# Two 32-column products in place of one 64-column product in the RWKV inverse of a diffusion trunk step

## The reference

```
sa = s @ kk_t
s  = s * w_t - outer(sa, kk_t * a_t) + outer(v_t, k_t)
y  = s @ r_t
```

## Time and profile before

| | before |
|---|---|
| runs, median (lowest to highest) | 3530.35 us (3522.43 to 3538.04) |
| the profiled execution | 3516.0 us |
| its span | 3514.2 us |
| PE busy, share of the span | 3166.6 us, 90% |
| DVE busy | 1607.5 us, 46% |
| ACT busy | 970.3 us, 28% |
| granted TensorE clock, mean | 0.904 |

### The profile page before, as it was taken

The page is one execution under the profiler, slowest core; times in us unless marked ns, Lnnn a source line. Parts: engine busy times, 40 slices in busy tenths (PEclk is TensorE's granted clock), DMA queues, the critical chain, the costliest instruction groups (busy, mean ns, idle before and its releaser), DMA issues.

```text
span 3514.2 us, 61754 instructions
## 1 busy us (share of the span) xinstructions
PE 3166.6 (90%) x26668; PEld 3001.6 (85%) x26668; DVE 1607.5 (46%) x2434; ACT 970.3 (28%) x1645; POOL 0.2 (0%) x4
## 2 busy tenths in 40 slices
PE   7799999986688887999999999999996777999998
PEld 7799999985476666999999999999984446999998
DVE  2454545644355544554555554546124433422323
ACT  1221212313343432321212312123224444321222
POOL 0000000000000000000000000000000000000000
PEclk6899999996688998999999999999996667999999
DMA  6244443200000002244433343433220001222221
GB/s 216 80 126 114 120 116 106 71 22 0 14 5 6 6 4 73 79 120 116 123 103 114 100 122 108 122 106 102 78 61 1 0 1 48 70 72 74 74 78 58
DMA packets 389633, 264.44 MB, mean 75 GB/s; under 512 B 11179, under 2 KB 370886, under 8 KB 389318
## 3 DMA queue, kind: packets, MB, share of 16 engines
q1 hardware_dynamic: 389446, 261.70, 26.2%
HBM read 257.61 MB, written 4.06 MB: 74 GB/s over the span
## 4 chain that ended last, share of the span: by engine, by line
PE 85%; DVE 8%; ACT 3%; issue 1%; DMA 1%; SPq 0%; ACTq 0%; DVEq 0%
PE banks L2433 62%; PE banks L1619 2%; PE banks L2456 2%; PE banks L2442 2%; PE banks L2387 2%; DVE w_lo_as_f L1828 1%; ACT h_lo_as_f L1733 1%; PE banks L1640 1%; PE banks L435 1%; PE banks L843 1%; PE banks L410 1%; PE banks L837 1%; PE banks L2463 1%; PE banks L826 1%; PE banks L898 1%
## 5 line engine op out<-in xcount | busy, mean ns | idle before, releaser
L2433 PE MATMUL banks<-h_hi,w_hi 128*128 128x320 f32 x3600 | 826.5, 311 | 19.8 <-DVE w_lo L2134 19.8
L2433 PE MATMUL banks<-h_lo,w_hi 128*128 128x320 f32 x3600 | 825.4, 311 | 0.0
L2433 PE MATMUL banks<-h_hi,w_lo 128*128 128x320 f32 x3600 | 825.1, 311 | 0.0
L2433 PEld LDWEIGHTS banks<-h_hi,w_hi 128*128 128x128 f32 x3600 | 606.7, 189 | 20.6 <-issue 20.6
L2433 PEld LDWEIGHTS banks<-h_lo,w_hi 128*128 128x128 f32 x3600 | 607.1, 189 | 0.0
L2433 PEld LDWEIGHTS banks<-h_hi,w_lo 128*128 128x128 f32 x3600 | 606.5, 189 | 0.0
L2433 PE MATMUL banks<-big_as_f32r,w_hi 128*128 128x320 f32 x2816 | 536.7, 313 | 4.7 <-DVE w_lo L2134 4.7
L2134 DVE TENSOR_TENSOR w_lo<-raw,w_hi 128x1024 fp32r<-128x1024 f32 x333 | 398.5, 1217 | 216.3 <-ACT w_hi L2018 215.7
L2018 ACT ACTIVATE w_hi<-raw 128x1024 fp32r<-128x1024 f32 x333 | 341.6, 1050 | 471.8 <-DMA raw<-ffn_w 248.8
L2433 PEld LDWEIGHTS banks<-big_as_f32r,w_hi 128*128 128x128 f32 x2816 | 449.5, 191 | 5.8 <-DVE w_lo L2134 5.5
L2279 DVE TENSOR_TENSOR work<-work,banks 128x640 f32<-128x640 f32 x88 | 72.3, 821 | 623.9 <-PE banks L2433 610.6
(11 more groups left out here) (351 smaller groups left out, 3033.2 us busy)
## 6 DMA issues: line engine op xcount, KB each, us to landing
raw<-ffn_w SPq DMA_DIRECT2D x272, 512.0 KB, 5.1
work<-mod_w SPq DMA_DIRECT2D x136, 512.0 KB, 3.8
raw<-w_in_c SPq DMA_DIRECT2D x24, 512.0 KB, 3.7
raw<-w_in_ab SPq DMA_DIRECT2D x21, 512.0 KB, 3.9
w_hi_as_f<-mod_w SPq DMA_DIRECT2D x8, 512.0 KB, 4.8
raw<-w_out_ab SPq DMA_DIRECT2D x8, 512.0 KB, 5.1
raw<-w_out_c SPq DMA_DIRECT2D x8, 512.0 KB, 6.3
h_hi_as_f<-x_sample SPq DMA_DIRECT2D x1, 2048.0 KB
```

What stands on the lines that cost most here:

```text
L2433: ins = nc.tensor.matmul(ps[:, c, 0:HALF], w, v[:, k, c * HALF:(c + 1) * HALF], start=(k == 0 and w is hi and v is xh), stop=(k == kts - 1 ...
```

## The change

Each call of P and of Q is split in two by its weight columns: instead of one call with 64 weight columns and 64 output partitions there are two with 32 weight columns and 32 output partitions. For each k the four quarters are gone round with the first 32 columns, then with the second 32. The moving side is the same for both. Output places, masks, semaphores and everything around stay as they are.

```
@@ level_p
                 for k in range(NCH):
-                    for e, p in quads:
-                        u = 2 * k + e
-                        ins = mm(bank(p)[heads[e], k * HL:(k + 1) * HL], w_u4[d][heads[p], u, 0, :],
-                                 split_cols(w_t, lev, hp)[heads[p], u], start=True, stop=True)
+                    for c in range(0, L, HL):
+                        for e, p in quads:
+                            u, o = 2 * k + e, e * L + c
+                            ins = mm(bank(p)[o:o + HL, k * HL:(k + 1) * HL], w_u4[d][heads[p], u, 0, c:c + HL],
+                                     split_cols(w_t, lev, hp)[heads[p], u], start=True, stop=True)
                 ins.then_inc(PL.sem(f"P{lev}"), 1)
@@ level_q
                 for k in range(NCH):
-                    for e, p in quads:
-                        ins = mm(bank(e)[heads[p], k * HL:(k + 1) * HL], tt[heads[e], k, p, :], pb[heads[e], p, k, :],
-                                 start=True, stop=True)
+                    for c in range(0, L, HL):
+                        for e, p in quads:
+                            o = p * L + c
+                            ins = mm(bank(e)[o:o + HL, k * HL:(k + 1) * HL], tt[heads[e], k, p, c:c + HL], pb[heads[e], p, k, :],
+                                     start=True, stop=True)
                 ins.then_inc(PL.sem(f"Q{lev}"), 1)
```

## The result

| | before | after |
|---|---|---|
| runs of one comparison, median (lowest to highest) | 3533.19 us (3522.43 to 3541.69), 8 runs | 3566.62 us (3547.18 to 3576.44), 8 runs |
| the profiled execution, its span | 3516.0, 3514.2 us | 3566.58, 3564.8 us |
| repeated later on one chip, median | 3529.72 us, 10 runs | 3566.52 us, 6 runs |

The ratio is 1.0093 (95% interval 1.0065 to 1.0121): 33 us slower. The repeat gave 1.0088 (1.0057 to 1.012) for the changed kernel and 0.9986 (0.9969 to 1.0003) for the kernel before against itself, both against 26 further runs of the kernel before with a median of 3535.03 us. P is now line 827, Q 840, X 846, the mask 1410 and the subtractions 1421.

What follows compares the result with a forecast made beforehand. PE's code supply, in blocks of 256 instructions, was taken as the bound. Product gain and tiling switches cancelled to 0, supply added 30 us: 3546 us for the profiled execution, 3560 against the 3530.35 median, range 3535 to 3594.

Steps and rivals of the forecast that it cites:

- The bound and the mechanism: PE stalls for code in blocks of 256 instructions; 6400 more make 25 more blocks, costing 30 us.
- D: Rival: standing still for code, PE gets the lower clock more often, 27 us on top of 30: 3587; chance 0.06.
- The product by itself: Load starts of one P or Q go from 0.57 us to 0.53, between 0.29 and 1.15; 3 us gained.
- Rival C: Instruction count limits P and Q: a product takes 1.15 us, the kernel 3584; chance 0.10.
- The changes of tiling: Switches between P or Q and scan or y_rows: 0.15 us each, 49 places, about 20 count, 3 us.
- The price of a block: Fastest supply of PE code: 3.3 us for 256 instructions, 12.9 ns each; spread 3.0 to 3.7 us.
- The levels: Stage's code shortfall per pass: level 1 0.4 us, 2 0.7, 3 and 4 none, 5 1.4; 20 us in all.
- my factor for unevenness: Addition for blocks cut unevenly across the 40 levels, raising the code supply loss from 20 us to 30.
- a quarter of the way up: Code supply loss set between a 20 us floor and 62 us with one short block per level: 30 us.
- A: Rival: code supply keeps up and narrow loads pay, 0.57 to 0.33 us a product: -17 us, 3513; chance 0.12.
- B: Rival: code supply keeps up and the product stays at 0.53 us: 0 to +3 us, 3531; chance 0.10.

Runs made afterwards that it cites:

- e_loop: Kernel before plus 640 small calls at the start of the stage, as a loop of 20 turns of 32 calls: 3547.53 us, ratio 1.0035.
- e_train: Kernel before plus 640 small calls (2560 PE instructions) written out at the start of the stage: 3562.14 us, ratio 1.0074.
- e_fill: Kernel before, unsplit, plus 40 small calls behind each Q, adding as many PE instructions as the change: 3565.64 us, ratio 1.0088.
- e_b32: Changed kernel with P and Q on bf16 upper halves of their operands, one pass, 80 instructions a product: 3520.24 us, ratio 0.9963.
- e_b64: Kernel before with P and Q on bf16 upper halves, unsplit, one pass, 40 instructions a product: 3515.02 us, ratio 0.9963.

## Why the prediction came out as it did

**The bound and the mechanism** were right. Code in blocks of 256 instructions, 25 more of them, 86 in the stage, stalls in X, P, Q and y_rows: all are there. e_loop against e_train shows that such stalls are the code, e_fill that as many instructions without the split lose as much, and e_b32 against e_b64 that the split with little code loses far less. The stalls themselves grew by 23 to 24 us. That leaves some 10 of the 33 us, which the sum had at nothing: a slightly lower clock in the runs (3 to 7 us, see D below), and for the rest the slower product and the changes of tiling are the candidates. This division is an estimate from the traces, and no run has that rest by itself.

**The product by itself** was taken at 0.53 us of starts, between 0.29 and 1.15, and is 0.67. I had one part of it right (each instruction doesn't keep its 7 ns), and the sign wrong: from 0.54 to 0.67 is a loss of 0.13 a product, not a gain of 0.04. At the full clock the narrow calls come at one instruction in 4.2 ns, and 160 of them need 0.67 us; the calls on constants of e_train and the bf16 ones of e_b32 come at the same pace once their first 33 loads are through. Only at the lower clock did 32 columns pay (0.80 us of starts against 0.94). The Trainium skill ("TensorE: Matmul & The Clock Gate", section on LDWEIGHTS) would have a product's loads halved by this change; at neither clock did they. Rival C has a small part in this; its price of 1.15 us a product is out. What the slower product costs in the end is open: 0.13 us on all 80 would be 10 us, and e_b32 against e_b64 leaves room for that. While a level waits for code, a slower product may be hidden in that wait, but that is argued and not shown.

**The changes of tiling** were taken at 0.15 us. Weight loads of the changed kernel, from P to the scan:

```profile
1087.46 0.78 PEld L827 LDWEIGHTS banks<-h_lo_as_f,work 64*32 64x32 f32 x80 [0.44 <-issue]
1088.28 0.19 PEld L805 LDWEIGHTS banks<-w_hi_as_f 64*64 64x64 f32 x3
```

P's loads end at 1088.24 and the scan's begin 0.04 us later, where they began 0.10 us early: 0.14. The price of one change was right; how many of them count was not measured. Level 5 of pass 2, where no stall fell, has both effects in it: 5.13 us from X to the step behind it, 4.83 before. So where code was not short, the split did cost, 0.30 us in this level.

**The price of a block** was taken at 3.3 us, with 3.7 as the slow end, and e_train gives 3.73. It was the mis-sized term of the supply. The two ends of the sum were also worked out wrong: with the prediction's own stretches, 3.0 us a block makes 8 us (not 5) and 3.7 makes 39 (not 45).

**The levels.** The distribution failed. Forecast, as a floor for eight passes: level 1 3.2 us, level 2 5.6, levels 3 and 4 nothing, level 5 11.2. Found, first traces: 14.1, 17.3, 2.5, 8.0 and 3.8. The error is in my stretches of the earlier trace rows: only the first runs from X to X. The one that I called level 2 ended 1.07 us late, and the one called level 5 began 1.04 us late and ended 0.39 early; levels 3 and 4 are shifted with them. The stretches from X to X, in before (levels 1, 2, 3 of pass 3; 4, 5 of pass 2), then in the changed kernel:

```profile
1104.60:1108.54 3.94, 2.99 (x94) 2.24 (x88) 3.80 (x8) 1.29 (x3) 0.00 (x0) 1.00 0.02 4
1108.54:1113.80 5.26, 4.58 (x180) 3.80 (x180) 3.10 (x8) 1.29 (x3) 0.00 (x0) 1.00 0.01 3
1113.80:1120.20 6.40, 4.62 (x111) 4.09 (x111) 2.29 (x8) 4.25 (x6) 0.00 (x0) 0.79 0.01 4
...
1075.07:1080.06 4.99, 4.31 (x106) 3.02 (x106) 2.65 (x7) 1.82 (x4) 0.00 (x0) 1.00 0.01 3
1080.06:1084.89 4.83, 4.75 (x118) 3.54 (x118) 1.58 (x6) 2.56 (x7) 0.00 (x0) 1.00 0.01 3
```
```profile
1123.22:1129.08 5.86, 3.52 (x174) 2.53 (x168) 3.91 (x8) 1.29 (x3) 0.00 (x0) 1.00 0.02 6
1129.08:1135.95 6.87, 5.33 (x259) 4.25 (x260) 3.10 (x8) 1.29 (x3) 0.00 (x0) 1.00 0.02 5
1135.95:1142.24 6.29, 5.64 (x192) 5.04 (x192) 2.31 (x8) 4.25 (x6) 0.00 (x0) 0.63 0.02 4
1090.58:1096.85 6.27, 4.79 (x185) 3.34 (x185) 2.65 (x7) 1.83 (x4) 0.00 (x0) 1.00 0.01 3
1096.85:1101.98 5.13, 5.13 (x197) 3.90 (x197) 1.57 (x6) 2.41 (x6) 0.00 (x0) 1.00 0.02 6
```

Level 2 is 360 records in 5.26 us, then 520. At 14.6 ns these need 7.6 us: +2.3 a pass. Level 1 with 334 needs 4.9: +0.9. Level 4 with 372: +0.4, level 5 with 396: +1.0, both counted in the three passes of eight that have these lengths (the levels that last 6.4 to 12.4 us have room, and the shorter ones of passes 0, 1 and 7 are left out). That is 7.5 + 14 to 19 (six to eight passes) + 1.3 + 2.9 = 26 to 30 us, without my factor for unevenness. The same sum for P alone (level 1: 254 need 3.7, nothing lost; level 2: 440 need 6.4, +1.2) gives 7 to 9 us where 10.8 and 8.3 were measured, and so would explain why the halves don't add up to the whole. It was worked out afterwards, from e_train's rate, and is an argument and not a test.

**The step "a quarter of the way up", from 20 to 30 us,** stood in for what I couldn't place. The floor with the right stretches at 12.9 ns would have been 17 us (level 1 0.4, level 2 1.5, level 5 0.3 a pass), so the guess carried a wrong cut and a block price that was too low. The total came out near because these errors and the 10 us above went against each other: 30 forecast, 33 measured. The mechanism was read right, but the closeness of the number is luck. Why level 1 lost 14 us where the rate asks for 7.5 stays open; it follows the dense front of the pass, which may leave the supply behind, but no run changed the front.

**The rivals.** A and B needed a supply that keeps up; 28 stalls where there were 6 rule them out. The Trainium skill ("Runtime: NRT & Kernel Launch", Instruction fetch mechanics) has the fetch hidden behind the issue rate and a PE buffer of 2048 instructions. Here PE stood after 474 instructions of e_train, and the fetch lasted 3.73 us a block where the issue took 1.4: the measurement decides. For D the granted clock of the stage fell from 0.89 to 0.83, but this is not the change: the repeat of the kernel before has 0.84 with the same code. Its levels took 13 us more than those of the first profile, and those of the changed kernel (263.5 us at 0.83) are still 32 us above them. The executions say the same. Those of the kernel before took 3542 us in the mean at a mean granted clock of 0.894 (7 runs) and 3529 at 0.899 (17 runs); the changed kernel took 3567 and 3570 at 0.894, and 3556 and 3562 at 0.899. At equal clock it is in the mean 26 and 30 us slower, so the clock has some 3 to 7 us of the 33, and whether the change brings that about is not shown. Level 3 of pass 3 went from 0.79 to 0.63 and got no longer (6.40 and 6.29 us). ACT is busy for 4.25 us of it in both, so another engine than PE may set its length. The range (3535 to 3594) held the time, and that of the repeat.

## What to carry to other kernels

Count instructions, not only array time: a change that keeps the work and doubles the calls of an unrolled PE stage pays for its code wherever the stage runs 256 instructions in less than some 3.7 us, and it pays in the dense stretches, not in those where PE waits for another engine anyway. Cut such stretches from one step of the loop to the same step of the next before a rate is set against them, and look at every pass: the room in a wait (2.3 to 5.6 us here) is no constant. A loop whose body is short brings the code once; where a stage is short of code, that or fewer calls are the ways to look at, not narrower ones.

## What the runs showed of the hardware

- PE's code: 3.73 us for 256 instructions in an unbroken run, with 474 instructions run before the first stall (e_train). A loop body of 128 instructions was not fetched again, and PE stood for 0.17 to 0.24 us at each turn (e_loop).
- Loads and matmuls of 32 columns came at one instruction in about 4.2 ns at the full clock where code was there; the first 33 loads of a product went in 0.16 us, and 0.11 us without a start came behind them.
- Halving a load's columns from 64 to 32 with twice the calls made a product slower at the full clock (loads 0.67 to 0.78 us) and quicker at half of it (1.16 to 0.95).
- The same kernel took 13 us more in its levels at a granted clock of 0.84 than at 0.89, so two single profiles don't measure a change of this size; many executions, compared at equal clock, do better.
- A change between 64x32 and 64x64 tiling delayed the next load by 0.14 us.
